# Attention block with branch keys rounded into weight slots: the third branch's keys in another slot, one output unit converted later

## What is computed

```python
qb = qk_norm(heads(q_b, B_HEADS), q_gain_b) * qscale
k_sel = qk_norm(heads(ks, B_KV), k_gain_sel)
k_win = qk_norm(heads(kw, B_KV), k_gain_win)
o_a = banded_gqa(qa, ka, heads(v_a, A_KV), SWA_WINDOW, rel_bias[:, :A_HEADS], sinks)
o_cmp, o_sel = nsa_cmp_sel(qb, k_cmp, v_cmp, k_sel, heads(vs, B_KV), bias_b)
o_win = banded_gqa(qb, k_win, heads(vw, B_KV), NSA_WINDOW, bias_b, None)
o_b = gb[..., 0, :] * o_cmp + gb[..., 1, :] * o_sel + gb[..., 2, :] * o_win
y = jnp.concatenate([o_a * silu(z_a), o_b * silu(z_b)], axis=-1)
out = x + gate[:, None, :] * (y @ w_out)
```

## Time and profile before

| what | value |
|---|---|
| median of 3 runs | 1461.34 us |
| the profiled execution, its own time | 1461.91 us |
| its span in the trace | 1460.2 us |
| PE busy | 1436.3 us, 98% of the span |
| DVE busy | 741.5 us, 51% |
| ACT busy | 601.3 us, 41% |
| POOL busy | 112.4 us, 8% |
| share of the chain that ended last | PE 95% |
| step 0 to the last scores | about 205 us to 312 us |
| load of one unit (512 KB), from issue to landing, median | 3.9 us |
| first unit run by `pe_unit` behind the attention (28) | from 324.87 us |

### The profile page before, as it was taken

The page is one execution under the profiler, slowest core; times in us unless marked ns, Lnnn a source line. Parts: engine busy times, 40 slices in busy tenths (PEclk is TensorE's granted clock), DMA queues, the critical chain, the costliest instruction groups (busy, mean ns, idle before and its releaser), DMA issues.

```text
span 1460.2 us, 18290 instructions
## 1 busy us (share of the span) xinstructions
PE 1436.3 (98%) x6990; PEld 1207.1 (83%) x6990; DVE 741.5 (51%) x1200; ACT 601.3 (41%) x1009; POOL 112.4 (8%) x131
## 2 busy tenths in 40 slices
PE   6999999999999999999999999999999999999998
PEld 5788879998888888888888888888888888888887
DVE  6741677855665533556455444453457333333332
ACT  5633577755343332333333444532355333333221
POOL 5302322210000000000000111100000000000000
PEclk9999999999999999999999999999999999999999
DMA  9995200123433333312223233344332333333321
GB/s 283 322 237 186 75 1 2 31 73 93 152 101 109 98 97 101 101 44 87 68 63 87 58 87 101 87 144 113 89 90 84 115 89 101 99 93 94 110 79 57
DMA packets 227825, 149.71 MB, mean 103 GB/s; under 512 B 5330, under 2 KB 216014, under 8 KB 227108
## 3 DMA queue, kind: packets, MB, share of 16 engines
q1 hardware_dynamic: 223588, 131.63, 31.2%
q0 software_dynamic: 4160, 17.04, 4.0%
HBM read 140.92 MB, written 6.68 MB: 101 GB/s over the span
## 4 chain that ended last, share of the span: by engine, by line
PE 95%; SPq 1%; DMA 1%; DVE 1%; ACT 1%; issue 1%; DVEq 0%; ACTq 0%
PE ps L433 70%; PE ps L2215 6%; PE ps L2241 3%; PE ps L1938 3%; PE ps L2140 3%; PE ps L1830 3%; PE ps L2227 1%; DMA w_raw<-in_w_in_dram 1%; PE ps L1961 1%; PE ps L1899 1%; PE ps L2126 1%; PE ps L2125 1%; SPq L547 1%; PE ps L1954 1%; SPq L577 0%
## 5 line engine op out<-in xcount | busy, mean ns | idle before, releaser
L453 DVE TENSOR_TENSOR w_lo<-w_raw,w_hi 128x1024 fp32r<-128x1024 f32 (+1 forms) x214 | 258.1, 1209 | 251.0 <-ACT w_hi L448 248.1
L448 ACT ACTIVATE w_hi<-w_raw 128x1024 fp32r<-128x1024 f32 (+1 forms) x214 | 219.4, 1034 | 15.3 <-PE ps L433 11.3
L499 ACT ACTIVATE temps<-ps 128x512 f32<-128x512 f32 x67 | 40.0, 597 | 238.9 <-PE ps L433 238.9
L433 PE MATMUL ps<-g_hi,w_hi 128*128 128x512 f32 x384 | 95.8, 392 | 0.0
L433 PE MATMUL ps<-g_hi,w_lo 128*128 128x512 f32 x384 | 94.9, 389 | 0.0
L433 PE MATMUL ps<-g_lo,w_hi 128*128 128x512 f32 x384 | 94.8, 389 | 0.0
L433 PEld LDWEIGHTS ps<-g_hi,w_lo 128*128 128x128 f32 x384 | 72.1, 188 | 15.0
L433 PEld LDWEIGHTS ps<-g_lo,w_hi 128*128 128x128 f32 x384 | 72.1, 188 | 14.9
L433 PEld LDWEIGHTS ps<-g_hi,w_hi 128*128 128x128 f32 x384 | 71.5, 188 | 14.6
L433 PE MATMUL ps<-f_lo,w_hi 128*128 128x512 f32 x288 | 71.1, 389 | 0.0
L433 PE MATMUL ps<-f_hi,w_hi 128*128 128x512 f32 x288 | 71.1, 389 | 0.0
(11 more groups left out here) (442 smaller groups left out, 2734.8 us busy)
## 6 DMA issues: line engine op xcount, KB each, us to landing
w_raw<-in_w_in_dram SPq DMA_DIRECT2D x107, 512.0 KB, 3.9
w_raw<-in_w_ff_gate_dram SPq DMA_DIRECT2D x22, 512.0 KB, 3.8
w_raw<-in_w_ff_up_dram SPq DMA_DIRECT2D x22, 512.0 KB, 3.8
w_ada_shift_scale<-in_w_ada_dram SPq DMA_DIRECT2D x16, 512.0 KB, 7.8
w_raw<-in_w_r_out_dram SPq DMA_DIRECT2D x16, 512.0 KB, 4.5
w_raw<-in_w_ff_down_dram SPq DMA_DIRECT2D x16, 512.0 KB, 4.2
w_ada_gate<-in_w_ada_dram SPq DMA_DIRECT2D x4, 1024.0 KB, 10.9
x_spill<-x_t POOLq DMA_DIRECT2D x2, 2048.0 KB, 9.0
```

The costliest lines, as they stand in the source:

```text
L433: mm = pe.matmul(bank, w[:, slot, k], mov[:, at_k], start=first and n == 0 and k == 0, stop=last and n == 2 and k == kts - 1)
L448: act.activation(whi[:, slot, 0:kts], raw[:, slot, 0:kts], ACT.Copy).then_inc(hi_done, 1)
L453: nc.vector.tensor_tensor(wlo[:, slot, 0:kts], raw[:, slot, 0:kts], whi[:, slot, 0:kts].bitcast(F32), ALU.subtract).then_inc(lo_done, 1)
L499: act.activation(dst, ps[:, o % 4], func, scale=scale).then_inc(evac, 1)
```

## The change

- `KW_SLOT` becomes `(U_LAST + AHEAD) % SLOTS` = 28 modulo 4 = 0, the slot of unit 24 (done before `U_LAST`) and of unit 28.
- ACT rounds pieces 0 and 1 of the third branch ahead of step 0, right behind the second branch's four; pieces 2 and 3 at s = 4 and 7.
- On DVE `head_norm` 9 and 10 come ahead of the four `k_local_rest`.
- Unit 28 is converted behind the last scores: ACT at s = 97, DVE at s = 99, both with a wait for all 96 scores. Unit 27 is converted by DVE at s = 61 as before.

```diff
-K_WINDOW_AT = (4, 6, 8, 9)
+K_WINDOW_AT = (4, 7)
...
-        KS_SLOT, KW_SLOT = (U_Z + GB_AT) % SLOTS, U_LAST % SLOTS
+        KS_SLOT, KW_SLOT = (U_Z + GB_AT) % SLOTS, (U_LAST + AHEAD) % SLOTS
...
-            for part in range(4):
-                k_round(1, part)
+            for b, parts in ((1, 4), (2, 2)):
+                for part in range(parts):
+                    k_round(b, part)
...
-                if s == CONVERT_AT:
+                if s == N_ATT + 1:
+                    act.wait_ge(m["s_mm"], N_ATT)
                     act_convert(act, None, 0, U_LAST + AHEAD)
                 if s in K_WINDOW_AT:
-                    k_round(2, K_WINDOW_AT.index(s))
+                    k_round(2, 2 + K_WINDOW_AT.index(s))
...
                 if n == 23:
                     compressed_softmax()
+                for t in BCAST_AT.get(n, ()):
+                    head_norm(t)
+                if n == 23:
                     for part in range(4):
                         k_local_rest(part)
-                for t in BCAST_AT.get(n, ()):
-                    head_norm(t)
...
-                if s in (CONVERT_AT, CONVERT_AT + 2):
-                    dve_convert(dve, None, 0, U_LAST + (s - CONVERT_AT) // 2 + 1)
+                if s == CONVERT_AT:
+                    dve_convert(dve, None, 0, U_LAST + 1)
...
+                if s == N_ATT + 3:
+                    dve.wait_ge(m["s_mm"], N_ATT)
+                    dve_convert(dve, None, 0, U_LAST + AHEAD)
                 for i, half in tails_at(s):
```

## The result

| | median of the device time | runs |
|---|---|---|
| before | 1461.37 us | 17 |
| changed | 1464.43 us | 17 |

The ratio is 1.002, with a 95% interval from 1.0014 to 1.0027: slower by 3.1 us. One of the 17 executions of the kernel before took 1605.86 us, a slow one that the ratio leaves out and that does not move the median. Forecast were +2.1 us and 1463.4 us, in a range from 1460.6 to 1465.3; it went the way that was forecast, 1 us further. The profiled execution of the changed kernel took 1464.31 us, with a span of 1462.6.

A forecast was written before the change was run, and what follows sets the result against it. TensorE (PE) was taken to bound the kernel, waiting only in the first two dozen steps and behind the last scores. +0.64 +0.99 -1.0 +0.6 +0.87 = +2.1 us gave a median of 1463.4 us, range 1460.6 to 1465.3.

The forecast's parts named there:

- the forecast's own branch: Whole kernel: some of the holds and the tail cost +1.0 to +3.0 us (1462.3 to 1464.3), chance 0.47.
- The six pieces ahead of step 0: ACT before step 0: two extra rounding pieces cost nothing, as starting earlier covers their 1.3 us.
- The start: DVE before step 0: POOL's earlier pieces hold the fourth local rest and the maximum, so step 0 comes 0.64 us later.
- the first-in-line reading: SBUF port before step 0: waiting POOL goes ahead of DVE's fourth rest, +0.64 us; if DVE kept the port, -0.4.
- L1418: DVE's coefficients of step 1: they stand behind POOL's sixth piece, +0.99 us.
- ACT's gain: ACT by step 12: rounding pieces leaving steps 8 and 9 win 1.3 us, a moved piece costs 0.3, so -1.0 us.
- the hold of the row sum: DVE at step 11: POOL's last rests hold the row sum between 0 and 1.15 us, taken as 0.6.
- The middle: Steps 61 and 63: taking unit 28's conversions out wins 0, as PE hides both.
- The tail: Behind the last scores: DVE's conversion of unit 28 waits for ACT's and delays the last output by 0.87 us.
- Rival 1: SBUF port: reordered work misses POOL's holds or DVE keeps the port, -0.5 to -0.1 us, 1461.0; chance 0.22.
- Rival 4: Behind the last scores: the tail is hidden while the holds come, +1.2 us, 1462.6; chance 0.05.
- Rivals 2 and 3: Granted clock near 225 us: falls more, +3.8 us, 1465.1, chance 0.18; or does not fall, 1459.1 to 1461.7, chance 0.08.

The follow-up runs named there:

- e11: The kernel before, unchanged, run again for its profile: 1461.69 against 1461.24 us, ratio 1.0001.
- e12: The changed kernel, unchanged, run again: 1464.35 us, ratio 1.0018 against before, +3.11 us.
- e8: Changed kernel with POOL starting no low part until the compressed probabilities are copied: 1464.73 against 1461.18 us for the kernel before, ratio 1.0024.
- e3: Kernel before with only the second and third branch's key norms moved ahead of the four local rests on DVE: 1461.75 against 1461.28 us, ratio 1.0004.
- e4: Changed kernel with POOL's third-branch rests waiting for DVE's first compressed output: 1463.35 against 1461.28 us for the kernel before, ratio 1.0015.
- e5: Changed kernel with ACT's last two pieces in steps 4 and 6 instead of 4 and 7: 1462.87 against 1461.18 us for the kernel before, ratio 1.0012.
- e6: Changed kernel with the edits of e2, e4 and e5 together: 1461.68 against 1461.18 us for the kernel before, ratio 1.0004.
- e1: Kernel before with only unit 28's conversion moved behind the last scores: 1462.46 against 1461.28 us, ratio 1.001.
- e2: Changed kernel with ACT's conversion of unit 28 at s = 96 instead of 97: 1462.58 against 1461.28 us for the kernel before, ratio 1.001.
- e9: Changed kernel with e2's and e5's edits, POOL starting behind the probabilities' copy, its third piece behind DVE's coefficients: 1461.49 against 1461.24 us before, ratio 0.9999.
- e10: e9 with the sink also added one step earlier for i = 1 to 3: 1461.83 us, +0.59 against the kernel before, ratio 1.0004.

## Why the prediction was right, and where it was off

The direction, the four places and the mechanism at each came as forecast; the size did not quite. By the medians the loss lies just above the forecast's own branch (+1.0 to +3.0) and above the 1464.26 us for which "slower by over 0.2%" had a chance of 0.21.

The differences of the profiles without a fall of the clock (e11 and e12) sum up to +2.83 us; the medians say +3.1.

- *The six pieces ahead of step 0 are free on ACT.* Right: the copy behind them moved by 0.05 us.
- *The start, +0.64 us.* Right: POOL did go ahead of the fourth rest, which took 1.67 us, as the first-in-line reading had it; the other reading, -0.4, is out. The maximum ends 8.89 us behind the start of the softmax's last subtraction, where it ended at 8.25: +0.64. Step 0 itself is only 0.50 late. In the kernel before it waited for its scores and not only for DVE: e8, where DVE is ready 1.1 us ahead of it, has it at the same 9.43 us. So the 1.19 us that the forecast laid from the maximum's end to step 0 held some of that wait, and were 1.03 (and 204.72 + 1.19 is 205.91, not 205.95). By step 1 the start has cost 0.62 to 0.65 after all (e3, e4, the changed kernel).
- *L1418, +0.99 us.* Right, a little large: +0.96 between step 0 and step 2; e4 puts 0.83 of it to POOL alone, which is what the coefficients take more (1.09 against 0.26 us), and the rest belongs to the start, which e3 shows at 0.62 by step 2.
- *ACT's gain of 1.0 us and the hold of the row sum, 0.6 us, together -0.4.* This is the step that failed by size: from step 2 to 13 it was +0.35. The hold came in full (1.02 us of duration, 0.86 on the path by e5), where I took half of it; and the pieces win 0.5, not 1.0, as e5 and e6 show. The bound I had named, +0.3 with the hold met in full, was near the value by luck: it is a hold of 1.3 less a gain of 1.0 (and 1.3 is more than the 1.15 us named for the hold itself), where the runs have 0.86 less 0.51. Why the gain is half I did not separate: the pieces cost ACT 2 x 0.65, and in e5, against step 2, step 10 still stands 0.28 us later than before, and only steps 12 and 13 win.
- *The middle, 0.* Right (e1: 15.33 against 15.30 us between steps 60 and 72).
- *The tail, +0.87 us.* Right: +0.94 or 0.95 from step 95 to the last output in every profile with this order, and nothing once ACT converts one step earlier (e1, e2). PE's wait is 1.05 us.
- *The later load of unit 32.* PE is busy for 278.00 of 278.00 us from 325 us on, as before: 0.

The sum with those sizes is 0.50 + 0.96 + 0.35 + 0.95 = 2.8. I was short by 0.7 us of that, and the pair of rounding and row sum, 0.75 too low, is all of it; the others cancel. Of the 0.75 some 0.5 are ACT's gain, put at twice its size, and 0.25 the hold. Rival 1 (the port is missed) is out by four held instructions. Rival 4 (the tail is hidden) is what e2 makes of it. Rivals 2 and 3 were about the clock: their fall of it exists, but it comes in single executions of either kernel (below), and it costs 1.1 us and not the 1.7 at which both had it. The medians differ from the distances by up to 0.5 us in either direction, and so do two equal kernels; nothing smaller is settled by them.

## What to carry to other kernels

When a part of a chain is moved to where its engine is idle, follow what that engine's result sets free: here ACT's spare time was real, but what it fed was POOL, and POOL's work fell on DVE's small two-operand instructions, which then hold up the pipeline for eight columns. Put work behind the last data of a stage only after looking at the order of both engines that touch it; one place earlier on ACT was the whole difference between 0.95 us and none. And before pricing a hold, look whether the engine that sets the end waits for it: 1.5 us of holds in steps 59 and 83 were worth 0.3, by the distances.

## What the runs showed of the hardware

- DVE instructions that follow each other with a gap of 0.04 us did not keep POOL out. In all seven profiles with the norms first and POOL free to start (changed, e2 to e6, e12) the fourth rest stood behind POOL's piece for a microsecond, 1.67 or 1.68 us instead of 0.69; in e8, where POOL starts later, it takes 0.69. By the Trainium skill (SBUF — State Buffer, Who interferes with whom) whoever issues first gets the pair of SBUF ports that DVE and POOL share for its whole instruction; the runs agree (1.67 us against 0.69).
- The same holds for instructions of hardly any size: a DVE operation of 8 columns with two operands in SBUF takes 0.16 or 0.17 us alone and 0.77 to 1.09 behind a POOL piece (row sums of steps 11 and 59, sink in e9).
- The granted clock fell to the lower level, 0.50, in 4 of 14 profiles: in the first of the kernel before, near 225 us, in e8 from 210 to 217 us, and in e9 and e10 near 225 us. The same kernel showed it once (before, 1461.91 us) and once not (e11). It costs 1.1 us by step 95 in the first profile of before (114.96 against 116.08) and in e9 as much, counted from step 13. Ahead of it PE had holes in every case (1.20 us busy of 2 in e8), but so had the other profiles, without a fall: in e11 PE is busy 1.45 us of 2 from 224 to 226 us, at 1.00. What sets it off stays open. So a trace of one execution is to be read for such a stretch before two traces are compared: against the first one, the change would seem to cost 1.64 us up to the last output and not 2.8.
